# Which expert rows the vector engine adds itself: one condition in the slot loop of a hybrid decoder layer

## The reference, cut to what matters

```python
e = i1[ci // 16] * 128 + i2[ci % 16]          # 8 heads x 16 chosen experts per token
gate = softmax(sc)
h = einsum('td,thkd->thk', xb, u[e])          # one dot product per token and expert
w = gate * gelu(h)
y = einsum('thk,thkd->td', w, v[e])           # weighted sum of expert rows
```

## Time and profile before

| | |
|---|---|
| time, median of 3 runs | 2162.49 us (2161.5 to 2168.59) |
| the profiled execution's own time | 2168.59 us |
| its span | 2166.8 us |
| PE busy | 1803.3 us (83%) |
| DVE busy | 1368.5 us (63%) |
| ACT busy | 780.0 us (36%) |
| POOL busy | 742.0 us (34%) |
| DMA | 771.86 MB, mean 356 GB/s |
| HBM read | 754.53 MB |

### The profile page before, as it was taken

The page is one execution under the profiler, slowest core; times in us unless marked ns, Lnnn a source line. Parts: engine busy times, 40 slices in busy tenths (PEclk is TensorE's granted clock), DMA queues, the critical chain, the costliest instruction groups (busy, mean ns, idle before and its releaser), DMA issues.

```text
span 2166.8 us, 20392 instructions
## 1 busy us (share of the span) xinstructions
PE 1803.3 (83%) x6195; PEld 892.1 (41%) x6195; DVE 1368.5 (63%) x2944; ACT 780.0 (36%) x2342; POOL 742.0 (34%) x646
## 2 busy tenths in 40 slices
PE   6899999878878798878779897878789989776877
PEld 3345454555433453534345353435433323453211
DVE  2562333298765788866578887667856545559654
ACT  3332122225363345436224544522423322223333
POOL 2110011033534444443434343443323323444542
PEclk9999999999989899989999999999979999988999
DMA  8573222389999999999999999999999999999998
GB/s 261 199 256 124 75 80 113 137 319 385 400 425 428 427 422 425 359 426 398 418 430 424 406 372 425 396 428 428 423 367 400 412 400 389 428 428 421 425 427 342
DMA packets 139112, 771.86 MB, mean 356 GB/s; under 512 B 14529, under 2 KB 23377, under 8 KB 61290
## 3 DMA queue, kind: packets, MB, share of 16 engines
q0 software_dynamic: 83680, 605.56, 68.0%
q1 hardware_dynamic: 52562, 160.11, 19.8%
q10 hardware_dynamic: 2760, 4.88, 0.6%
HBM read 754.53 MB, written 16.26 MB: 356 GB/s over the span
## 4 chain that ended last, share of the span: by engine, by line
PE 40%; DMA 29%; DVE 15%; ACT 7%; issue 4%; POOL 2%; SPq 1%; ACTq 0%; DVEq 0%; POOLq 0%
DMA sb_uv<-in_peer_uv,sb_eidx 24%; PE bank L1992 17%; PE bank L1629 8%; DVE sb_uv L1594 6%; DMA sb_zone<-in_cache_kT 3%; PE bank L1903 2%; PE bank L1961 2%; PE bank L1937 2%; PE bank L1882 1%; ACT sb_diag L1215 1%; POOL sb_uv L880 1%; DVE sb_hres L1571 1%; ACT sb_ew L1208 1%; ACT L1204 1%; DMA pre_conv<-sb_raw 1%
## 5 line engine op out<-in xcount | busy, mean ns | idle before, releaser
L1992 PE MATMUL bank<-sb_uv,sb_diag 128*128 128x512 f32 (+1 forms) x1860 | 951.1, 646 | 280.0 <-ACT sb_diag L1215 271.3
L880 POOL DMA_INDIRECT sb_uv<-in_peer_uv,sb_eidx x576 | 673.8, 1170 | 1042.5 <-PE bank L1992 816.4
L1594 DVE CUSTOM_DVE_ANT_0 sb_uv<-sb_uv,sb_xn 128x1024 f32<-128x1024 f32 x576 | 699.4, 1221 | 330.3 <-DMA sb_uv<-in_peer_uv,sb_eidx 327.6
L1992 PEld LDWEIGHTS bank<-sb_uv,sb_diag 128*128 128x128 f32 (+1 forms) x1860 | 331.3, 194 | 768.7 <-ACT sb_diag L1215 425.2
L1204 ACT ACTIVATE sb_gel<-sb_h 128x1 f32<-128x1 f32 x576 | 116.3, 202 | 881.7 <-DVE sb_h L1594 880.0
L1629 PE MATMUL bank<-sb_w,sb_xnT 128*128 128x512 f32 (+1 forms) x560 | 259.6, 612 | 4.0 <-ACT sb_qkn L932 4.0
L1215 ACT ACTIVATE sb_diag<-sb_stay,sb_ew 128x128 f32<-128x128 f32 (+1 forms) x465 | 183.2, 394 | 43.4 <-ACT sb_ew L1208 0.7
L1208 ACT ACTIVATE sb_ew<-sb_gel,sb_gate 128x1 f32<-128x1 f32 x576 | 169.7, 295 | 19.8
L1961 PEld LDWEIGHTS bank<-sb_rT,sb_zone 128*128 128x128 f32 x1280 | 157.2, 197 | 28.8 <-issue 28.3
L1571 DVE SCALAR_TENSOR_TENSOR sb_hres<-sb_uv,sb_ew,sb_hres 128x1024 f32<-128x1024 f32 x111 | 142.2, 1281 | 35.2 <-ACT sb_ew L1208 35.0
L1961 PE MATMUL bank<-sb_rT,sb_zone 128*128 128x128 f32 x1280 | 158.3, 280 | 1.1 <-issue 0.8
(11 more groups left out here) (326 smaller groups left out, 1542.6 us busy)
## 6 DMA issues: line engine op xcount, KB each, us to landing
sb_zone<-in_w_route SPq DMA_DIRECT2D x20, 2304.0 KB, 12.3
sb_zone<-in_w_mixer SPq DMA_DIRECT2D x10, 2048.0 KB, 18.2
sb_zone<-in_cache_kT SPq DMA_DIRECT2D x64, 256.0 KB, 9.8
sb_zone<-in_cache_v SPq DMA_DIRECT2D x64, 256.0 KB, 9.5
sb_w<-in_w_sections SPq DMA_DIRECT2D x28, 512.0 KB, 5.2
sb_uv<-in_peer_uv,sb_eidx POOLq DMA_INDIRECT x576, 11.5
sb_hres<-pre_conv SPq DMA_DIRECT2D x4, 1024.0 KB
sb_zone<-pre_conv SPq DMA_DIRECT2D x4, 1024.0 KB, 5.3
```

What stands on the lines that cost most here:

```text
L880: nc.gpsimd.indirect_dma_start(uv[:, m % RING, :], None, i["peer_uv"], bass.IndirectOffsetOnAxis(ap=eidx[:, t % 2, n:n + 1], axis=0)).then ...
L1594: nc.vector.tensor_tensor_reduce(out=uv[:, m % RING, 0:D], in0=uv[:, m % RING, 0:D], in1=xn2[:, t % 2, :], scale=1.0, scalar=0.0, op0=ALU. ...
L1992: ins = nc.tensor.matmul(bank[half][0:rows, :], lhsT=G["diag"][:, d % DIAGS, 0:rows], rhs=uv[:, m % RING, D + 512 * half:D + 512 * half + ...
```

## The change

For tiles 0 to 2 another set of slots goes to DVE. In tile 3 nothing changes.

```diff
         def added_here(m):
             t, n = ALL[m]
-            return t < PT and n % 5 in (1, 4) and (t + 1 == PT or 33 <= n < 50 or 72 <= n < 105)
+            return t < PT and n % 5 in (1, 4) and (t + 1 == PT or 45 <= n < 105)
```

## The result

The changed kernel takes 2190.02 us in the median of 5 runs (2189.07 to 2192.32). The kernel before took 2167.10 us in its 5 runs. The ratio is 1.0118, with a 95% interval of 1.0100 to 1.0136: 23 us slower by the medians. The forecast was slower by 10, to 2172, within 2158 to 2183. So the direction was as forecast, and the size was less than half of what came. The profiled execution has a span of 2188.8 us, 22.0 more than before.

What follows compares the result with a forecast made beforehand. The DMA was taken as the main bound, losing time only where its queue runs dry. Part 1's 6.6 us plus Part 2's 3.8 gave 10.4 on the median of 2162.5: 2172.9, stated as 2172, range 2158 to 2183.

Steps and rivals of the forecast that it cites:

- Part 1: GDN stretch, tiles 0 to 2: five slots a tile go to PE; 6.6 us slower, between 0 and 13.5.
- I take 2.2 us: GDN stretch: gather 48 lands late by 2.2 us a tile, chosen from 1.5 or 3.6.
- The bound of three late gathers: GDN stretch: at most 1.5 us more for each gather that meets the 8.2 us landing; 4.5 a tile.
- Part 2: Attention, tiles 0 to 2: nine slots a tile go to DVE; 3.8 us slower, between -8.2 and +7.3.
- the 0.7 of the first head: Attention, first head: the adds of slots 51 and 54 fall mostly into waits and cost 0.7 us.
- the hole at gather 69: DMA hole in attention, released by slot 62 on PE; grows by 2.7 us in tile 1, 2.0 in tile 2.
- The relief of 0.9: Slots 63 to 72: PE has four slots fewer; 0.9 us taken back once.
- tile 2's 2.0: Attention, tile 2: the longer head cycle costs 2.0 us, as the first head's adds hide behind data.
- Gather 69 starts 9 us or more behind 68.: Attention: a sign that would show the forecast right; the distance before was 7 us.
- It cancels: Rival: GDN's queue is deep enough, PE's relief returns attention's loss; about +1 us, 2163.5; chance 0.27.
- PE's relief wins: Rival: DVE returns buffers sooner, attention's end stays fed, GDN costs nothing; -8.2 us, 2154.3; chance 0.15.
- The adds hold up more: Rival: lengthened POOL gathers and half clock in tiles 0 and 2 add 7 us, 2180; chance 0.08.

Runs made afterwards that it cites:

- Part 1 alone: Kernel before, with slots 34, 36, 39, 41 and 44 of tiles 0 to 2 moved to PE: 1.0061, 2180.3 against 2166.0 us.
- slot 41 alone: Kernel before, with only slot 41 of tiles 0 to 2 moved to PE: 1.0014 (0.9995 to 1.0034).
- PE's load alone: Kernel before, all adds kept on DVE, PE doing two extra constant matmuls for each of slots 34, 36, 39, 41, 44: 1.0045.
- the five head adds alone: Kernel before, with only slots 51, 54, 56, 59 and 61 of tiles 0 to 2 moved to DVE: 1.0049 (1.0031 to 1.0068).
- the end adds alone: Kernel before, with only slots 64, 66, 69 and 71 of tiles 0 to 2 moved to DVE: 1.0007 (0.9993 to 1.0020).
- with slot 62: Kernel before, with slot 62 of tiles 0 to 2 also moved to DVE: 1.0001; with slot 57 moved too: 0.9999.
- fourteen kernels: The kernel before (2167.10 us), the changed kernel (2190.02 us) and the twelve kernels of the experiments, none of which beats the kernel before.
- the changed kernel with PE's extra matmuls: Changed kernel, PE doing two extra constant matmuls for each slot from 51 to 71 that went to DVE: 1.0081, 2189.2 us.
- The one version that shortened the cycle: Changed kernel, with the adds of slots 51 to 71 of tiles 0 to 2 one slot later in DVE's order: 1.0093, 2188.0 us.
- three experiments: Kernel before, tiles 0 to 2, moved to DVE: slots 38, 43, 48 (1.0000); slots 64, 66, 69, 71 (1.0007); slot 62 (1.0001).

## Why the prediction was wrong, point by point

- **What bounds the kernel.** Right in the main. The time goes with the DMA's dry stretches: 26.9 us more are lost in the six, and the span is 22.0 us longer. But the sum is no finer than some 7 us, by which it moves between kernels of equal time. (At 425 GB/s a gather is worth 2.47 us, not 2.45; no sum uses it.)
- **Part 1, the mechanism.** Up to gather 48 it went as forecast: the chunk ends 4.8 us later (4.8), gather 48 starts 9.1 us later (8.3), takes 5.7 us (6.1) and lands 1.9 us late (1.5 to 3.6). Only its distance to gather 47 is off, 5.9 where about 8 was forecast, because gather 47 was itself 4.8 us late; the forecast's own "2 to 4 us later" for it would have given 5.8 to 7.8. PE had no idle time from slot 33 to 44, where the forecast had said to 48. The Trainium skill's figure for such a transfer (DMA: Bandwidth & Descriptors, Anatomy of one DMA: 2.0 us plus bytes/436e3) gave an estimate of 5.4 with POOL's part; the measured 5.7 lies between it and the 6.1.
- **Part 1, the size: the step that failed.** "I take 2.2 us" a tile. The runs show about 4: 3.7, 4.1 and 3.4 more lost, and 13 us in all with Part 1 alone (8 to 18 by its interval). The step priced one buffer, the one whose releaser changed, and counted gathers 45 to 47 as "still inside the queue". But the queue was nearly used up by then (gather 45 lands in 6.8 us, close to the 6.1 of a dry queue), slot 41 alone adds only 0.3 us of lost DMA time in three tiles, and PE's load alone brings all of it (11.5 us). Five slots are 9.55 us of work in a stretch in which PE had 4.6 us idle (44.3 less 39.7), so everything PE releases there comes late. The GDN stretch got 4.3 to 5.1 us longer in each tile. The bound of three late gathers, 4.5 a tile and 13.5 in all, was nearer than the value taken.
- **Part 2, the cycle.** Right: 11.3 and 10.8 us against 11.3 and 10.9 forecast. The first distance, 10.8, fits the 0.7 of the first head, but by luck: with the five head adds alone it stays at 10.08.
- **Part 2, what the cycle costs: the second step that failed.** 3.8 us forecast, at most 7.3, and 11 measured (7 to 15). Two terms of the sum were too small. Tile 0 was counted at 0, at most 2.6: it loses 3.6. Its gather 69 starts 36.5 us behind the first head's L1443 where it was 32.2 (648.94 - 612.44 and 644.65 - 612.49 in the timelines), 4.3 later, and the lead it had was the 8.7 us that it took to land less the 6.1 of a dry queue, 2.6. Tile 1 was counted at 2.7 by the hole at gather 69: it loses 4.8, as the hole at gather 69 moved with the gathers ahead of it and a second one opened at gather 65. The relief of 0.9 is too small to be seen: the end adds alone give 1.0007 (0.9993 to 1.0020). For tile 2's 2.0 no run gives a measure.
- **The range.** Part 1's 13 us are within its bound of 13.5, Part 2's 11 are beyond its 7.3. Even both upper bounds together, 20.8, are below the 23 measured.
- **"Gather 69 starts 9 us or more behind 68."** Wrong: 7.6. Gather 68 itself came late, because slot 61's add on DVE released it.
- **The rivals.** "It cancels" and "PE's relief wins" fell, the latter also in the runs with the end adds alone and with slot 62. "The adds hold up more" gave the nearest time, 2180, but that is luck, as it came by means that the runs don't bear out: a gather's mean on POOL went from 1170 to 1175 ns, and with the clock back at 0.87 to 0.89 the second hole stayed. The Trainium skill's rule on DVE and GpSimd sharing SBUF access (SBUF — State Buffer, "The single rule") is thus neither borne out nor refuted here: 12 more adds with two inputs changed the sum over 576 gathers by 2.9 us, and the lowest sum of all fourteen kernels, 665.0 us, is that of one with 123 adds (the changed kernel with PE's extra matmuls).
- **Open.** Why the losses add up to 5 us more than the span grew, how much of tile 2's loss belongs to the change, and how the 11 us of Part 2 divide between the cycle and late buffers. The one version that shortened the cycle gave back 2 us of the median (2190.0 to 2188.0), or 5 by the ratios (1.0118 to 1.0093), and both lie within the intervals. What PE's lower clock is worth is open too, by a few us.

## What to carry to other kernels

Where an engine has 2 us idle in a 34 us stretch, adding 9.6 us of work makes it the bound: price the length of the whole stretch and every buffer that the engine gives back in it, not the one buffer whose releaser changed. In a ring with gathers in a fixed order, a delay of the cycle shows at each release behind each head, and the lead of a tile that loses nothing must be compared with the delay before it is called safe. Relief of PE, or an earlier release of one buffer, gave nothing back that could be told in three experiments (1.0000, 1.0007, 1.0001). And a median within an interval of 7 us is no proof of "costs nothing": there the lost DMA time of the stretch said more than the time.

## What the runs showed of the hardware

- This kernel, which runs on one core, drew 425 and 426 GB/s over tens of microseconds (426 over 67.4 us in tile 0).
- Gather 48 of tile 1 (1.05 MB) landed after 12.9 us in the kernel before and after 5.7 in the changed one, where the queue was nearly dry. Over all 576 gathers of the kernel before this time is 5.5 to 23.7 us, 11.5 in the median.
- POOL's gather instruction took 0.94 us in many rows but 1.7 to 2.0 in others. The longer ones stand often, though not only, behind a release by DVE (1.69, idle 1.80). Over all 576 the mean hardly moved, 1154 to 1191 ns in the fourteen kernels, and no experiment tried what lengthens them.
